# Two layer norms behind expert layers: some statistics moved to ScalarE, mean and gain in one VectorE operation

## The chip, the cores and the metric

One core of a Trainium2 chip runs the whole program. The metric is the device time of one execution in microseconds. The engines are TensorE (PE in the profile), VectorE (DVE), ScalarE (ACT), GpSimd (POOL) and SyncE (SP), which issues transfers; each runs its own instructions in program order, and they wait for one another by semaphores.

## What is computed

The reference is a decoder trunk of two layers over 1040 tokens (16 meta tokens and 1024 of the input) of width 1024. Layer 0 mixes by a convolution and a sparse attention, layer 1 by a gated recurrence. Behind each mixer comes a routed expert layer, and everything is wrapped in a norm behind the sum:

```python
for layer in range(DEPTH):
    m = conv_sparse_attn_mixer(h, ...) if layer % 2 == 0 else rglru_mixer(h, ...)
    h = layer_norm(DN_ALPHA * h + m, ln_mix_g[layer], ln_mix_b[layer])
    f = hierarchical_moe(h, ...)
    h = layer_norm(DN_ALPHA * h + f, ln_ffn_g[layer], ln_ffn_b[layer])
return h[:, N_META:]

def layer_norm(x, g, b):
    mu = jnp.mean(x, axis=-1, keepdims=True)
    var = jnp.mean(jnp.square(x - mu), axis=-1, keepdims=True)
    return (x - mu) * lax.rsqrt(var + LN_EPS) * g + b
```

The two norms with `ln_ffn` are those of this change.

## The kernel before

The program is a row of stages with a barrier of all engines between them. The expert layers leave their sums (already `h + f / ALPHA`) in DRAM; `combine` reads them in blocks of 128 tokens and norms them. It is called twice in `trunk`:

- c0 (L2712), behind layer 0's experts: nine blocks (the first has 16 tokens, the others 128), `turned` is true. The normed rows are stored and also transposed by TensorE, and each transposed block is split into a high part (`high`, ScalarE, L2386) and a low part (`low`, VectorE, L2354) for the products of the next stage. The two halves of the PSUM that take the transposes are used in turn (`TURN_SETS` = 2), so the transposes of block n wait for `low` of block n - 2. ScalarE and GpSimd also split the first two weight tiles of the recurrence (`odd.split_hi`, L2274, and `odd.split_lo`, L2278), and TensorE does the 24 steps (three matmuls each) of odd tile 0 between and behind the transposes (`STEPS_BEHIND`, L2256): 4 steps behind each of blocks 5, 6 and 7, 12 behind block 8. Steps 8 to 15 wait for `low` of block 6, steps 16 to 23 for that of block 8. The recurrence begins when all engines are through.
- c1 (L2721), the end of the kernel: eight blocks of 128 tokens, `turned` is false. The normed rows are the output.

The rows of the first two blocks are loaded ahead of the barrier, the others as the stage begins (L1738). For block n, VectorE does two `bn_stats` of 512 columns (L2333), `bn_aggr` (L2335) and adds EPS (L2336); ScalarE takes the root (`root`, L2378); VectorE takes the reciprocal (L2340) and -mean times it (L2341, together `scale`); ScalarE computes x * scale + bias in place (`centre`, L2382); VectorE multiplies by the gain, which ScalarE has copied to PSUM (`gain`, L2346, with L2389); GpSimd adds the bias (L2408); SyncE stores the rows (L2323). In c1 VectorE adds the bias of the last block itself (L2350, from a copy in PSUM, L2391).

The order is written out by hand. In turn n of its loop VectorE does stats(n), scale(n - 1), gain(n - 2) and, in c0, low(n - 4). ScalarE does root(n), centre(n - 1) and, in c0, high(n - 3). `Chain.link` makes VectorE wait for its own small results.

Of the kernel before, what the change touches and what calls it, by code (L numbers as in the profile page):

```python
# [14 lines left out]
ALU = mybir.AluOpType  # L15
ACT = mybir.ActivationFunctionType
# [7 lines left out]
P = 128  # L24
D = 1024
# [19 lines left out]
ALPHA = float(4 ** 0.25)  # L45
EPS = 1e-5
# [29 lines left out]
def tok0(b):  # L76

    return 0 if b == 0 else META + P * (b - 1)


def toks(b):
    return META if b == 0 else P
# [819 lines left out]
N = len(STEPS)  # L902
# [812 lines left out]
class Sums:  # L1715
# [11 lines left out]
    def gain(self, j):  # L1727
        return self.raw[:, GAIN_CHUNK, j * D:(j + 1) * D]
# [556 lines left out]
                   (hT_hi[:, k, m], hT_lo[:, k, m]), k == 0, k == KC - 1)  # L2285


def combine(nc, name, const, sums, out_d, hT_hi, hT_lo, beside=None, odd=None):


    blocks, x = sums.blocks, sums.rows
    N = len(blocks)
    turned = hT_hi is not None
    with Ctx(nc) as c:
        stat = c.sb(name + "st", [P, N, 18])
        g_ps = odd.bank[:, 6:8, :] if turned else c.ps(name + "g", [P, 2, 512])
        t_ps = [odd.bank[:, 2 + 2 * s:4 + 2 * s, :] for s in range(TURN_SETS)] if turned else [c.ps(name + "t", [P, 2, 512])]
        stored, bias_in, last_normed = c.sem(name + "so"), c.sem(name + "bin"), c.sem(name + "lnd")
        chain, padded, gain_in, var_done, root_done, scales, centred, gained, normed, t_mm, hi_d, lo_d = (
            c.sem(name + n) for n in ("ch", "pad", "gin", "vd", "rtd", "scl", "cen", "gain", "nd", "tm", "hd", "ld"))  # L2300
        block = c.block()

        def col(n, a, w=1):
            return stat[0:toks(blocks[n]), n, a:a + w]

        def turns(n):
            return t_ps[n % TURN_SETS].rearrange("p a (j n) -> p (a j) n", j=4)[:, :, 0:toks(blocks[n])]

        def hT(t, n):
            return t[:, :, tok0(blocks[n]):tok0(blocks[n]) + toks(blocks[n])]  # L2310

        @block.sync
        def _(sp):
            sums.load_rows(sp, BEHIND_CHANGE)
            if beside is not None:
                beside(sp)
            for n, b in enumerate(blocks):
                at = tok0(b) - sums.out0
                if n < N - 1 or turned:
                    sp.wait_ge(normed, n + 1)  # L2320
                else:
                    sp.wait_ge(last_normed, 1)
                sp.dma_start(out_d[at:at + toks(b), :], x(n)).then_inc(stored, 16)  # L2323
            sp.wait_ge(stored, 16 * N)

        @block.vector
        def _(dve):
            ch = Chain(dve, chain)

            def stats(n):  # L2330
                dve.wait_ge(sums.loaded[n], 16)
                for j in range(2):
                    ins = dve.bn_stats(col(n, 6 * j, 6), x(n)[:, 512 * j:512 * j + 512])  # L2333
                ch.link(ins)
                ch.link(dve.bn_aggr(col(n, 12, 2), col(n, 0, 12)))  # L2335
                dve.tensor_scalar(col(n, 14), col(n, 13), EPS / ALPHA ** 2, None, ALU.add).then_inc(var_done, 1)  # L2336

            def scale(n):
                dve.wait_ge(root_done, n + 1)
                ch.link(dve.reciprocal(col(n, 16), col(n, 15)))  # L2340
                dve.tensor_scalar(col(n, 17), col(n, 12), col(n, 16), -1.0, ALU.mult, ALU.mult).then_inc(scales, 1)  # L2341

            def gain(n):
                dve.wait_ge(centred, n + 1)
                g = g_ps[0:toks(blocks[n]), :, :].rearrange("p a n -> p (a n)")
                dve.tensor_tensor(x(n), x(n), g, ALU.mult).then_inc(gained, 1)  # L2346
                if n == N - 1 and not turned:
                    dve.wait_ge(gained, N)
                    dve.wait_ge(bias_in, 1)
                    dve.tensor_tensor(x(n), x(n), t_ps[0][:].rearrange("p a n -> p (a n)"), ALU.add).then_inc(last_normed, 1)  # L2350

            def low(n):
                dve.wait_ge(hi_d, n + 1)
                dve.tensor_tensor(hT(hT_lo, n), turns(n), hT(hT_hi, n).bitcast(F32), ALU.subtract).then_inc(lo_d, 1)  # L2354

            if turned:
                dve.memset(hT_hi[:, :, T:TP].bitcast(F32), 0.0).then_inc(padded, 1)
                dve.memset(hT_lo[:, :, T:TP].bitcast(F32), 0.0).then_inc(padded, 1)
            for n in range(N + 4):
                if n < N:  # L2360
                    stats(n)
                if 1 <= n <= N:
                    scale(n - 1)
                if n == 2:
                    dve.wait_ge(gain_in, 1)
                if 2 <= n <= N + 1:
                    gain(n - 2)
                if turned and n >= 4:
                    low(n - 4)
            if turned:  # L2370
                dve.wait_ge(padded, 2)
                dve.wait_ge(lo_d, N)

        @block.scalar
        def _(act):
            def root(n):
                act.wait_ge(var_done, n + 1)
                act.activation(col(n, 15), col(n, 14), ACT.Sqrt).then_inc(root_done, 1)  # L2378

            def centre(n):  # L2380
                act.wait_ge(scales, n + 1)
                act.activation(x(n), x(n), ACT.Identity, bias=col(n, 17), scale=col(n, 16)).then_inc(centred, 1)  # L2382

            def high(n):
                act.wait_ge(t_mm, n + 1)
                act.activation(hT(hT_hi, n), turns(n), ACT.Copy).then_inc(hi_d, 1)  # L2386

            act.wait_ge(sums.gains_loaded, 32)
            act.activation(g_ps[:].rearrange("p a n -> p (a n)"), sums.gain(0), ACT.Copy).then_inc(gain_in, 1)  # L2389
            if not turned:  # L2390
                act.activation(t_ps[0][:].rearrange("p a n -> p (a n)"), sums.gain(1), ACT.Copy).then_inc(bias_in, 1)  # L2391
            for n in range(N + 3):
                if n < N:
                    root(n)
                if 1 <= n <= N:
                    centre(n - 1)
                if turned and n in (5, N):
                    odd.split_hi(act, n // N)
                if turned and n >= 3:
                    high(n - 3)  # L2400

        @block.gpsimd
        def _(pool):
            pool.wait_ge(sums.gains_loaded, 32)
            n_here = N if turned else N - 1
            for n in range(n_here):
                pool.wait_ge(gained, n + 1)
                pool.tensor_tensor(x(n), x(n), sums.gain(1)[0:toks(blocks[n]), :], ALU.add).then_inc(normed, 1)  # L2408
                if turned and n in (4, N - 1):
                    odd.split_lo(pool, n // (N - 1))  # L2410
            pool.wait_ge(normed, n_here)
            if turned:
                pool.wait_ge(odd.lo_done, 2)

        if turned:
            @block.tensor
            def _(pe):
                for n in range(N):
                    q = toks(blocks[n])
                    pe.wait_ge(normed, n + 1)  # L2420
                    if n >= TURN_SETS:
                        pe.wait_ge(lo_d, n - TURN_SETS + 1)
                    for k in range(KC):
                        last = pe.transpose(t_ps[n % TURN_SETS][:, k // 4, (k % 4) * P:(k % 4) * P + q], x(n)[:, k * P:(k + 1) * P],
                                            const[0:q, C_ID:C_ID + q])
                    last.then_inc(t_mm, 1)
                    for i in range(sum(STEPS_BEHIND.get(m, 0) for m in range(n)), sum(STEPS_BEHIND.get(m, 0) for m in range(n + 1))):
                        if i == 0:
                            pe.wait_ge(odd.lo_done, 1)
                        if i % KC == 0:  # L2430
                            pe.wait_ge(lo_d, BLOCKS_OF[i // KC])
                        if i == 2 * KC:
                            pe.wait_ge(padded, 2)
                        last = odd.step(pe, 0, i, hT_hi, hT_lo)
                last.then_inc(odd.tile_mm, 1)
# [373 lines left out]
```

## Time and profile before

| | |
|---|---|
| median of 3 runs | 2654.3 us (2651.59 to 2655.76) |
| the profiled execution | 2650.81 us |
| its span, mean granted TensorE clock | 2649.0 us, 0.958 |
| c0, first `bn_stats` to the last `low` | 1483.76 to 1525.90 us |
| c1, first `bn_stats` to GpSimd's last addition | 2615.86 to 2642.97 us |

In the rows below a time is in microseconds from the start of the span. A line such as L2346 is the line of the kernel. An instruction's row has its start, its duration, its engine, and in brackets how long the engine had been idle and who released it. Rows with x2 merge two instructions of a kind.

### The profile page before, as it was taken

To read this page: it belongs to the slowest core of one execution; us is meant where nothing else is said; L and a number is where in the kernel's file an instruction comes from. 1 tells how busy PE (TensorE), PEld (TensorE's weight loads), DVE (VectorE), ACT (ScalarE), POOL (GpSimd) and SP (SyncE) were. 2 spreads that over 40 slices of the span, in tenths; PEclk is the share of its full clock that TensorE was granted. 3 is DMA by queue.
4 is the path that set the end of the run, shared out by engine and by line. 5 is a ranking of instruction groups with operands and counts; after the bars stand their busy time and mean duration, and the time that the engine had idled before them with its cause. 6 is when DMAs were issued, how large, how long until landed. Compare 5 with 4: busy or idle time off the path is not lost. (4 is left out here: it accounts for less than half of the span.)

```text
span 2649.0 us, 37690 instructions
## 1 busy us (share of the span) xinstructions
PE 2429.4 (92%) x12633; PEld 2077.0 (78%) x12633; DVE 2022.3 (76%) x2597; ACT 1699.5 (64%) x1819; POOL 665.4 (25%) x487
## 2 busy tenths in 40 slices
PE   8989988986988999999999599997979999999993
PEld 8869967885776888888888489996867888888882
DVE  4688775677888898898898543536789889889885
ACT  2369836766216877778777465663157777877873
POOL 0105717752012212222212412120012222222223
PEclk9999999997998999999999699998979999999996
DMA  5503333313339699999798511104359699999994
GB/s 172 135 1 96 80 99 103 105 34 113 125 109 376 233 339 362 370 345 322 278 366 307 185 49 40 41 17 162 96 206 355 229 350 363 363 372 363 370 356 151
DMA packets 115278, 565.24 MB, mean 213 GB/s; under 512 B 23520, under 2 KB 27872, under 8 KB 65904
## 3 DMA queue, kind: packets, MB, share of 16 engines
q1 hardware_dynamic: 89776, 512.19, 53.0%
q0 software_dynamic: 25408, 51.84, 7.2%
q8 instruction: 53, 0.87, 0.1%
q14 instruction: 41, 0.34, 0.0%
HBM read 574.25 MB, written 74.34 MB: 245 GB/s over the span
## 5 line engine op out<-in xcount | busy, mean ns | idle before, releaser
L2047 DVE TENSOR_TENSOR e0wlo<-e0raw,e0whi 128x2048 fp32r<-128x2048 f32 x214 | 486.6, 2289 | 68.7 <-ACT e0whi L1902 67.2
L2047 DVE TENSOR_TENSOR e1wlo<-e1raw,e1whi 128x2048 fp32r<-128x2048 f32 x208 | 472.7, 2288 | 66.6 <-ACT e1whi L1902 66.5
L1902 ACT ACTIVATE e0whi<-e0raw 128x2048 fp32r<-128x2048 f32 x214 | 409.7, 1915 | 98.1 <-PE e0u L93 42.1
L1902 ACT ACTIVATE e1whi<-e1raw 128x2048 fp32r<-128x2048 f32 x208 | 397.9, 1915 | 94.0 <-PE e1u L93 42.1
L91 PE MATMUL odd_banks<-h2T_hi,odd_w_hi 128*128 128x348 f32 x480 | 171.6, 357 | 2.2 <-PEq L123 1.7
L92 PE MATMUL odd_banks<-h2T_lo,odd_w_hi 128*128 128x348 f32 x480 | 155.2, 323 | 0.0
L93 PE MATMUL odd_banks<-h2T_hi,odd_w_lo 128*128 128x348 f32 x480 | 154.9, 323 | 0.0
L91 PE MATMUL m_y<-m_whi,m_xhi 128*128 128x512 f32 (+1 forms) x304 | 123.4, 406 | 24.1 <-DVE m_wlo L1609 22.9
L93 PE MATMUL m_y<-m_whi,m_xlo 128*128 128x512 f32 (+1 forms) x304 | 120.3, 396 | 0.0
L92 PE MATMUL m_y<-m_wlo,m_xhi 128*128 128x512 f32 (+1 forms) x304 | 120.0, 395 | 0.0
L91 PE MATMUL e0g<-e0whi,e0xh 128*128 128x512 f32 x284 | 116.1, 409 | 3.2 <-DVE e0xl L2052 3.2
L91 PE MATMUL e0u<-e0whi,e0xh 128*128 128x512 f32 x292 | 115.6, 396 | 0.0
L92 PE MATMUL e0u<-e0wlo,e0xh 128*128 128x512 f32 x292 | 115.4, 395 | 0.0
L93 PE MATMUL e0u<-e0whi,e0xl 128*128 128x512 f32 x292 | 115.3, 395 | 0.0
L91 PE MATMUL e1g<-e1whi,e1xh 128*128 128x512 f32 x276 | 112.2, 406 | 2.6 <-DVE e1xl L2052 2.6
L91 PE MATMUL e0yp<-e0whi,e0hh 128*128 128x512 f32 x280 | 113.6, 406 | 0.0
L2278 DVE TENSOR_TENSOR odd_w_lo<-odd_w_raw,odd_w_hi 128x1024 fp32r<-128x1024 f32 x18 | 22.3, 1239 | 119.5 <-ACT odd_w_hi L2274 119.5
L93 PE MATMUL e0g<-e0whi,e0xl 128*128 128x512 f32 x284 | 112.8, 397 | 0.0
L92 PE MATMUL e0g<-e0wlo,e0xh 128*128 128x512 f32 x284 | 112.8, 397 | 0.0
L91 PE MATMUL e1u<-e1whi,e1xh 128*128 128x512 f32 x284 | 112.4, 396 | 0.0
L92 PE MATMUL e1u<-e1wlo,e1xh 128*128 128x512 f32 x284 | 112.2, 395 | 0.0
L93 PE MATMUL e1u<-e1whi,e1xl 128*128 128x512 f32 x284 | 112.2, 395 | 0.0
(477 smaller groups left out, 7069.5 us busy)
## 6 DMA issues: line engine op xcount, KB each, us to landing
e0raw<-in_moe_w_gate SPq DMA_DIRECT2D x72, 1024.0 KB
e0raw<-in_moe_w_up SPq DMA_DIRECT2D x72, 1024.0 KB
e0raw<-in_moe_w_down SPq DMA_DIRECT2D x72, 1024.0 KB
e1raw<-in_moe_w_gate SPq DMA_DIRECT2D x70, 1024.0 KB
e1raw<-in_moe_w_up SPq DMA_DIRECT2D x70, 1024.0 KB
e1raw<-in_moe_w_down SPq DMA_DIRECT2D x70, 1024.0 KB
qki_w_raw<-in_w_even SPq DMA_DIRECT2D x22, 512.0 KB, 5.8
odd_w_raw<-in_w_odd SPq DMA_DIRECT2D x20, 512.0 KB, 3.5
```

Of the source, the lines that this page charges most:

```text
L91: pe.matmul(out, stat[0], mov[0], start=start, stop=False)
L92: pe.matmul(out, stat[0], mov[1], start=False, stop=False)
L93: return pe.matmul(out, stat[1], mov[0], start=False, stop=stop)
L1902: act.activation(w_hi[:, i, :], raw[:, i, :], ACT.Copy).then_inc(hi_done[i], 1)
L2047: dve.tensor_tensor(w_lo[:, i, :], raw[:, i, :], w_hi[:, i, :].bitcast(F32), ALU.subtract).then_inc(lo_done[i], 1)
L2278: eng.tensor_tensor(self.w_lo[:, n % 2, :], self.raw[:, n % 2, :], self.w_hi[:, n % 2, :].bitcast(F32), ALU.subtract).then_inc(self.lo_don ...
```

## The change

- Of every three blocks, the third (n % 3 == 2) has its statistics on ScalarE: `sums_of` copies the rows to a scratch tensor with the sum in an accumulator; `squares` turns the sum into -mean, squares x - mean with the sum in the accumulator, and takes the root.
- The others keep `bn_stats` and `bn_aggr` on VectorE. EPS is now the bias of the root on ScalarE, from a small tensor that VectorE fills once.
- `gain` now comes ahead of the scaling: one `scalar_tensor_tensor` computes (x - mean) * g (or (x + -mean) * g) and needs no root. `scale` is the reciprocal alone. ScalarE's `centre` becomes `rescale`, x times the reciprocal, and waits for both; GpSimd's addition waits for `rescale`.
- The last block of c1 is not rescaled on ScalarE: `last_rows` computes x * scale + bias on VectorE in one operation.
- The order: in turn n VectorE does stats(n), gain(n), scale(n) and, in c0, low(n - 2). ScalarE does root(n), squares(n + 1) where n % 3 == 1, rescale(n), sums_of(n + 2) where n % 3 == 0 and, in c0, high(n - 2). The copy of the bias to PSUM in c1 moves into turn 1. The first `odd.split_hi` comes behind high(3), the second behind high(6).

```diff
+LOW_BEHIND = 2
+        ours = [n for n in range(N) if n % 3 != 2]
...
             def stats(n):
                 dve.wait_ge(sums.loaded[n], 16)
                 for j in range(2):
-                    ins = dve.bn_stats(col(n, 6 * j, 6), x(n)[:, 512 * j:512 * j + 512])
-                ch.link(ins)
-                ch.link(dve.bn_aggr(col(n, 12, 2), col(n, 0, 12)))
-                dve.tensor_scalar(col(n, 14), col(n, 13), EPS / ALPHA ** 2, None, ALU.add).then_inc(var_done, 1)
+                    dve.bn_stats(col(n, 6 * j, 6), x(n)[:, 512 * j:512 * j + 512]).then_inc(halves_done, 1)
+                dve.wait_ge(halves_done, 2 * ours.index(n) + 2)
+                dve.bn_aggr(col(n, 12, 2), col(n, 0, 12)).then_inc(var_done, 1)
+
+            def gain(n):
+                g = g_ps[0:toks(blocks[n]), :, :].rearrange("p a n -> p (a n)")
+                if n in ours:
+                    dve.wait_ge(var_done, ours.index(n) + 1)
+                    dve.scalar_tensor_tensor(x(n), x(n), col(n, 12), g, ALU.subtract, ALU.mult).then_inc(gained, 1)
+                else:
+                    dve.wait_ge(act_root_done, n + 1 - sum(m < n for m in ours))
+                    dve.scalar_tensor_tensor(x(n), x(n), col(n, 17), g, ALU.add, ALU.mult).then_inc(gained, 1)
 
             def scale(n):
-                dve.wait_ge(root_done, n + 1)
-                ch.link(dve.reciprocal(col(n, 16), col(n, 15)))
-                dve.tensor_scalar(col(n, 17), col(n, 12), col(n, 16), -1.0, ALU.mult, ALU.mult).then_inc(scales, 1)
-
-            def gain(n):
-                dve.wait_ge(centred, n + 1)
-                g = g_ps[0:toks(blocks[n]), :, :].rearrange("p a n -> p (a n)")
-                dve.tensor_tensor(x(n), x(n), g, ALU.mult).then_inc(gained, 1)
...
+                if n in ours:
+                    dve.wait_ge(root_done, ours.index(n) + 1)
+                dve.reciprocal(col(n, 16), col(n, 15)).then_inc(scales, 1)
...
-            for n in range(N + 4):
-                if n < N:
+            for n in range(N):
+                if n in ours:
                     stats(n)
-                if 1 <= n <= N:
-                    scale(n - 1)
-                if n == 2:
+                if n == 0:
                     dve.wait_ge(gain_in, 1)
-                if 2 <= n <= N + 1:
-                    gain(n - 2)
-                if turned and n >= 4:
-                    low(n - 4)
+                gain(n)
+                scale(n)
+                if turned and n >= LOW_BEHIND:
+                    low(n - LOW_BEHIND)
+            if not turned:
+                last_rows(N - 1)
...
-            def centre(n):
-                act.wait_ge(scales, n + 1)
-                act.activation(x(n), x(n), ACT.Identity, bias=col(n, 17), scale=col(n, 16)).then_inc(centred, 1)
+            def sums_of(n):
+                act.wait_ge(sums.loaded[n], 16)
+                act.activation(junk[0:toks(blocks[n]), :], x(n), ACT.Copy, accum_out=col(n, 12)).then_inc(sum_done, 1)
+
+            def squares(n):
+                k, q = n // 3 + 1, toks(blocks[n])
+                act.wait_ge(sum_done, k)
+                act.activation(col(n, 17), col(n, 12), ACT.Copy, scale=-1.0 / D).then_inc(mean_done, 1)
+                act.wait_ge(mean_done, k)
+                act.activation(junk[0:q, :], x(n), ACT.Square, bias=col(n, 17), accum_out=col(n, 13)).then_inc(square_done, 1)
+                act.wait_ge(square_done, k)
+                act.activation(col(n, 15), col(n, 13), ACT.Sqrt, bias=eps[0:q, :], scale=1.0 / D).then_inc(act_root_done, 1)
...
+            def rescale(n):
+                act.wait_ge(gained, n + 1)
+                act.wait_ge(scales, n + 1)
+                act.activation(x(n), x(n), ACT.Copy, scale=col(n, 16)).then_inc(scaled, 1)
+
+            act.wait_ge(eps_in, 1)
+            for n in range(N):
+                if n in ours:
                     root(n)
-                if 1 <= n <= N:
-                    centre(n - 1)
-                if turned and n in (5, N):
-                    odd.split_hi(act, n // N)
-                if turned and n >= 3:
-                    high(n - 3)
+                if n % 3 == 1 and n + 1 < N:
+                    squares(n + 1)
+                if turned or n < N - 1:
+                    rescale(n)
+                if n % 3 == 0 and n + 2 < N:
+                    sums_of(n + 2)
+                if turned and n >= 2:
+                    high(n - 2)
+                    if n in (5, N - 1):
+                        odd.split_hi(act, n // (N - 1))
...
-                pool.wait_ge(gained, n + 1)
+                pool.wait_ge(scaled, n + 1)
```

## Rows read from the trace of the kernel before

**Rows 1.** The page: TensorE's busy time over the span.
```profile
PE 2429.4 (92%) x12633; PEld 2077.0 (78%) x12633; DVE 2022.3 (76%) x2597; ACT 1699.5 (64%) x1819; POOL 665.4 (25%) x487
```

**Rows 2.** Timeline of c1, one period: start, duration, engine, operation.
```profile
2625.84 1.28 DVE L2333 BATCH_NORM_STATS2 c1st<-e1raw 128x6 f32<-128x512 f32 x2
...
2628.91 1.28 DVE L2333 BATCH_NORM_STATS2 c1st<-e1raw 128x6 f32<-128x512 f32 x2
2629.08 2.34 POOL L2408 TENSOR_TENSOR e1raw<-e1raw 128x1024 f32<-128x1024 f32 x1 [0.73 <-DVE e1raw L2346]
```

**Rows 3.** Timeline of c1: its start, block 2's statistics, GpSimd's last additions.
```profile
2615.86 1.28 DVE L2333 BATCH_NORM_STATS2 c1st<-e1raw 128x6 f32<-128x512 f32 x2 [19.98 <-PEq L123]
...
2619.69 1.28 DVE L2333 BATCH_NORM_STATS2 c1st<-e1raw 128x6 f32<-128x512 f32 x2
...
2638.30 4.67 POOL L2408 TENSOR_TENSOR e1raw<-e1raw 128x1024 f32<-128x1024 f32 x2 [0.73 <-DVE e1raw L2346]
```

**Rows 4.** Timeline of c0, VectorE, one period.
```profile
1505.56 1.28 DVE L2333 BATCH_NORM_STATS2 c0st<-e0raw 128x6 f32<-128x512 f32 x2
1506.87 0.21 DVE L2335 BATCH_NORM_AGGREGATE c0st<-c0st 128x2 f32<-128x12 f32 x1
...
1508.63 1.22 DVE L2354 TENSOR_TENSOR h2T_lo<-odd_banks,h2T_hi 128x1024 fp32r<-128x1024 f32 x1
...
1509.76 1.27 DVE L2333 BATCH_NORM_STATS2 c0st<-e0raw 128x6 f32<-128x512 f32 x2
```

**Rows 5.** Timeline of c0: its start, and its last high, low and step.
```profile
1483.76 1.25 DVE L2333 BATCH_NORM_STATS2 c0st<-e0raw 16x6 f32<-16x512 f32 x2
...
1523.61 1.03 ACT L2386 ACTIVATE h2T_hi<-odd_banks 128x1024 fp32r<-128x1024 f32 x1 [1.77 <-PE odd_banks L2424]
...
1524.67 1.23 DVE L2354 TENSOR_TENSOR h2T_lo<-odd_banks,h2T_hi 128x1024 fp32r<-128x1024 f32 x1 [1.57 <-ACT h2T_hi L2386]
...
1529.73 0.32 PE L93 MATMUL odd_banks<-h2T_hi,odd_w_lo 128*128 128x348 f32 x1
```

**Rows 6.** Waits in c0: total us, times, longest.
```profile
DVE h2T_lo L2354 <- ACT h2T_hi L2386: 4.5, 3, 1.6
```

**Rows 7.** Groups by form: busy us, mean ns of one, idle before.
```profile
L2382 ACT ACTIVATE e0raw<-e0raw,c0st 128x1024 f32<-128x1024 f32 x8 | 9.9, 1239 | 0.7
...
L2527 ACT ACTIVATE rg_t<-rg_r,const 128x1040 f32<-128x1040 f32 x10 | 11.6, 1157 | 0.0
...
L1245 ACT ACTIVATE pr<-sm,nmx 128x1040 f32<-128x1040 f32 x8 | 9.2, 1154 | 0.0
...
L1245 ACT ACTIVATION_READ_ACCUMULATOR pr<-sm,nmx 128x1 f32 x64 | 12.3, 192 | 0.0
...
L1224 ACT ACTIVATE conv_spare<-glu 128x1040 f32<-128x1040 f32 x4 | 4.3, 1071 | 0.5 <-issue 0.2 <-DVE glu L1346 0.2
...
L2378 ACT ACTIVATE c0st<-c0st 128x1 f32<-128x1 f32 x8 | 1.6, 202 | 7.6 <-DVE c0st L2336 7.6
...
L1408 DVE SCALAR_TENSOR_TENSOR m_rows<-m_rows,m_st,m_gb 128x1024 f32<-128x1024 f32 x8 | 10.2, 1275 | 0.0
...
L2346 DVE TENSOR_TENSOR e0raw<-e0raw,odd_banks 128x1024 f32<-128x1024 f32 x8 | 9.7, 1210 | 0.0
```

**Rows 8.** TensorE at both clocks: timeline of c0, then slices: length, busy, granted clock.
```profile
1511.61 1.97 PE L2424 MATMUL odd_banks<-const,e0raw 128*128 128x128 f32 x8 [2.66 <-POOL e0raw L2408]
...
1514.54 0.49 PE L92 MATMUL odd_banks<-h2T_lo,odd_w_hi 128*128 128x348 f32 x1
...
1514.83 0.49 PE L93 MATMUL odd_banks<-h2T_hi,odd_w_lo 128*128 128x348 f32 x1
...
1522.54 1.04 PE L2424 MATMUL odd_banks<-const,e0raw 128*128 128x128 f32 x8
...
338.00:340.00 2.00, 0.27 (x2) 1.00 0.00 0
...
342.00:344.00 2.00, 0.00 (x0) 0.71 0.00 0
```

More of the change, by code:

```diff
@@ L2295, in combine @@
         stat = c.sb(name + "st", [P, N, 18])
+        junk, eps = c.sb(name + "junk", [P, D]), c.sb(name + "eps", [P, 1])
+        ours = [n for n in range(N) if n % 3 != 2]
         g_ps = odd.bank[:, 6:8, :] if turned else c.ps(name + "g", [P, 2, 512])
@@ L2298, in combine @@
         stored, bias_in, last_normed = c.sem(name + "so"), c.sem(name + "bin"), c.sem(name + "lnd")
-        chain, padded, gain_in, var_done, root_done, scales, centred, gained, normed, t_mm, hi_d, lo_d = (
-            c.sem(name + n) for n in ("ch", "pad", "gin", "vd", "rtd", "scl", "cen", "gain", "nd", "tm", "hd", "ld"))
+        padded, gain_in, eps_in, halves_done, var_done, sum_done, mean_done, square_done = (
+            c.sem(name + n) for n in ("pad", "gin", "epi", "hvd", "vd", "smd", "mnd", "sqd"))
+        root_done, act_root_done, scales, scaled, gained, normed, t_mm, hi_d, lo_d = (
+            c.sem(name + n) for n in ("rtd", "ard", "scl", "scd", "gain", "nd", "tm", "hd", "ld"))
         block = c.block()
@@ L2327, in _ @@
         def _(dve):
-            ch = Chain(dve, chain)
             def stats(n):
@@ L2343, in gain @@
-            def gain(n):
-                dve.wait_ge(centred, n + 1)
-                g = g_ps[0:toks(blocks[n]), :, :].rearrange("p a n -> p (a n)")
-                dve.tensor_tensor(x(n), x(n), g, ALU.mult).then_inc(gained, 1)
[L2347 to L2350, printed above, removed]
+                    dve.bn_stats(col(n, 6 * j, 6), x(n)[:, 512 * j:512 * j + 512]).then_inc(halves_done, 1)
@@ new lines, in scale, with last_rows @@
+            def scale(n):
+                if n in ours:
+                    dve.wait_ge(root_done, ours.index(n) + 1)
+                dve.reciprocal(col(n, 16), col(n, 15)).then_inc(scales, 1)
+            def last_rows(n):
+                dve.wait_ge(gained, N)
+                dve.wait_ge(scales, N)
+                dve.wait_ge(bias_in, 1)
+                dve.scalar_tensor_tensor(x(n), x(n), col(n, 16), t_ps[0][:].rearrange("p a n -> p (a n)"), ALU.mult, ALU.add
+                                         ).then_inc(last_normed, 1)
@@ L2354, in low @@
                 dve.tensor_tensor(hT(hT_lo, n), turns(n), hT(hT_hi, n).bitcast(F32), ALU.subtract).then_inc(lo_d, 1)
+            dve.memset(eps[:], EPS / ALPHA ** 2).then_inc(eps_in, 1)
             if turned:
@@ L2358, in _ @@
                 dve.memset(hT_lo[:, :, T:TP].bitcast(F32), 0.0).then_inc(padded, 1)
-            for n in range(N + 4):
-                if n < N:
+            for n in range(N):
+                if n in ours:
                     stats(n)
-                if 1 <= n <= N:
-                    scale(n - 1)
-                if n == 2:
+                if n == 0:
                     dve.wait_ge(gain_in, 1)
-                if 2 <= n <= N + 1:
-                    gain(n - 2)
-                if turned and n >= 4:
-                    low(n - 4)
+                gain(n)
[4 more added lines that the diff above has]
+                last_rows(N - 1)
             if turned:
+                for n in range(N - LOW_BEHIND, N):
+                    low(n)
                 dve.wait_ge(padded, 2)
@@ L2376, in root @@
             def root(n):
-                act.wait_ge(var_done, n + 1)
-                act.activation(col(n, 15), col(n, 14), ACT.Sqrt).then_inc(root_done, 1)
-            def centre(n):
-                act.wait_ge(scales, n + 1)
-                act.activation(x(n), x(n), ACT.Identity, bias=col(n, 17), scale=col(n, 16)).then_inc(centred, 1)
+                act.wait_ge(var_done, ours.index(n) + 1)
+                act.activation(col(n, 15), col(n, 13), ACT.Sqrt, bias=eps[0:toks(blocks[n]), :]).then_inc(root_done, 1)
+            def sums_of(n):
[9 more added lines that the diff above has]
+                act.activation(col(n, 15), col(n, 13), ACT.Sqrt, bias=eps[0:q, :], scale=1.0 / D).then_inc(act_root_done, 1)
             def high(n):
@@ L2389, in _ @@
             act.activation(g_ps[:].rearrange("p a n -> p (a n)"), sums.gain(0), ACT.Copy).then_inc(gain_in, 1)
[L2390 to L2393, printed above, removed]
-                    root(n)
-                if 1 <= n <= N:
-                    centre(n - 1)
-                if turned and n in (5, N):
-                    odd.split_hi(act, n // N)
-                if turned and n >= 3:
-                    high(n - 3)
+            def rescale(n):
[5 more added lines that the diff above has]
+                if n in ours:
+                    root(n)
+                if n % 3 == 1 and n + 1 < N:
[8 more added lines that the diff above has]
+                        odd.split_hi(act, n // (N - 1))
+                elif not turned and n == 1:
+                    act.activation(t_ps[0][:].rearrange("p a n -> p (a n)"), sums.gain(1), ACT.Copy).then_inc(bias_in, 1)
+            if turned:
+                high(N - 2)
+                high(N - 1)
         @block.gpsimd
```

## The prediction

> **What bounds the kernel now.** I read the page's engine busy times first: TensorE is busy for 92% of the span [rows 1]. That share belongs to the projections and experts. The change touches only the two `combine` calls, c0 (behind layer 0's experts) and c1 (the end), so I read the timelines of these two stretches and asked which engine never rests.
>
> In c1 it is VectorE: its next `bn_stats` starts 3.07 us after the last one, without a gap, while GpSimd rests 0.73 us before each of its additions [rows 2]. Eight blocks at that pace, then GpSimd's last two additions back to back, end at 2642.97 [rows 3]. The chain of the end is VectorE's work and then GpSimd's, so what VectorE saves in c1 shortens the kernel.
>
> In c0 a period is 4.20 us, because each turn also has a `low` of 1.22 us (L2354) [rows 4]. VectorE waits for ScalarE before `low` only three times, 4.5 us together [rows 6]; these are the last three blocks. The last `low` ends at 1525.90, and TensorE's last step of odd tile 0 ends 4.15 us later, at 1530.05; everything behind it waits for that [rows 5].
>
> **What the change removes and adds on VectorE.** Per block with its own statistics go the operation that adds EPS (L2336), the product of mean and scale (L2341) and the plain product with the gain (1.21 us, L2346). In their place comes one `scalar_tensor_tensor` with a column pointer. The nearest row is L1408, the same operation with both tensors in SBUF, at 1.275; with the gain in PSUM and no pointer it is 1.21 [rows 7]. I take 1.275 (same kind), with 1.21 as the lower end. A turn of VectorE is then: 1.31 from the first `bn_stats` to the aggregate [rows 4], 0.24 for the aggregate and its wait, 1.20 for the product (0.08 overlaps its successor), 0.07 for the reciprocal: 2.8 us. A third block needs only 1.3 us. The `memset` of eps is under 0.1 us, once.
>
> **On ScalarE.** The rescale keeps one pointer: 1.16 us for 1040 elements (L2527), so about 1.14 for 1024, against 1.24 now (the upper end) [rows 7]. The next instruction starts 0.10 before its end: 1.04. Each third block adds a sum (an ACTIVATE of about 1.14 with its accumulator read of 0.19 [rows 7], 1.12 in the queue), and then a small copy, a square (1.07 for 1040 elements without the accumulator, 1.15 for an ACTIVATE with it), a read and a root, each waiting for the one before: 1.7 us [rows 7]. GpSimd's addition now follows the rescale, with the same 2.35 us.
>
> **c1.** Laid out in program order with these durations: blocks 0 and 1 take VectorE 2.81 us each from 2615.9; block 2 is 2.58 (VectorE waits 1.3 for the square's root, since ScalarE does root 1, mean, square and root one after another); blocks 3 to 5 are 2.81 + 2.81 + 2.58 = 8.2 where three blocks now are 9.2; blocks 6 and 7 are 2.81 and 2.9; the last scale-and-add is 1.28. VectorE ends at 2639.3 and GpSimd's seventh addition at 2639.2, against 2642.97: **-3.7 us**. What is late next is all three engines together (GpSimd alone needs 7.0 of the 8.2). The row loads are no limit: block 2's rows were there at 2619.7, where VectorE read them without a wait [rows 3], and ScalarE wants them at 2619.9.
>
> **c0.** Here I find a new ring, because `low` moves from four blocks behind to two and `high` from three to two. In turn n ScalarE's queue is root(n), rescale(n), `high`(n-2), and rescale(n) waits for VectorE's product and reciprocal of the same turn. VectorE's next instruction is `low`(n-2), which waits for `high`(n-2). Behind this `low` on VectorE stand the statistics and product of n+1, and for those ScalarE, GpSimd and TensorE wait. So the two engines take turns instead of overlapping. A turn becomes 1.31 + 0.24 + 1.20 + 0.18 (reciprocal and hand-over), then ScalarE's 1.04 (rescale) and 1.05 (`high`, 1.03 [rows 5], and hand-over), then 1.14 (`low`): 6.16. With the sum ahead of `high` (n = 3, 6) it is 6.16 + 1.12 = 7.28. With the square ahead of the rescale (n = 4, 7) the rescale starts 1.70 instead of 1.38 after the aggregate: 6.47. Without statistics (n = 5, 8) it is 4.61. Three turns: 18.4 us, against 12.6 now. GpSimd and TensorE have slack: a block's transposes end before ScalarE comes to its `high`.
>
> From 1483.8: turns 0 and 1 are 2.81 each, turn 2 is 4.23 (`low`(0) is short), turns 3 to 8 are 2 x 18.4: `low`(6) ends at 1530.5. Then TensorE's steps 8 to 11, which wait for it (12 matmuls at 0.16, 1.9), transposes of block 8 (1.04 [rows 8]), `high` and `low` with hand-overs (2.4): the last `low` ends at 1535.8 instead of 1525.9: **+9.9 us**. The same way of laying out the kernel before gives 1525.94 for that `low` and 2642.85 for GpSimd's last addition, 0.1 from the trace.
>
> **TensorE's clock in c0.** At the low level (0.50 granted, 1.2 GHz) a transpose group of eight takes 1.97 us and matmuls start 0.29 apart; at the high one (2.4 GHz) 1.04 and 0.16 [rows 8]. In the laid-out c0 TensorE works from 1525.1 to 1530.5 for only 1.0 us. Elsewhere it had 0.27 us of work in a 2 us slice at 1.00, and in the slice that began 2 us behind that one, without work, the grant fell (0.71) [rows 8]. I expect a fall here too: steps 8 to 11 then take 3.5 instead of 1.9, the transposes up to 1.97 instead of 1.04: **+2.5 us**, and by the time of the last eight steps TensorE has worked long enough to be back. The Trainium skill's page "TensorE: Matmul & The Clock Gate", section "Part 1: The HAM clock gate", says it this way: "the default state is throttled, and activity releases the throttle"; it speaks against a change that spreads TensorE's work thinner, and by a reading without it the time would be 2.5 us less.
>
> **Sum.** -3.7 + 9.9 + 2.5 = +8.7. The profiled execution took 2650.8 us, so its like would take 2659.5; the median of the three runs is 3.5 us above it, so the forecast is 2654.3 + 8.7 = **2663.0**. Bounds of the single costs: rescale 1.24 (+0.8 in c0, +0.2 in c1), product 1.21 (-0.4, and -0.3 in c1), accumulating ACTIVATEs 0.1 either way (0.5 either way): about 1.5 us down or up.
>
> **Rivals.** (A) The grant doesn't fall: 2660.5. For: matmuls come back after at most 3.3 us of rest. (B) It falls and stays low through the last eight steps: 24 matmuls at 0.29 instead of 0.16, +3.1: 2666.1. (C) The other side: VectorE never waits in `low`, since `high` is there early. Then c0 is bound by VectorE's own work, 10.5 per three turns instead of 12.6, some -5.9, and with c1's -3.7 it is 2644.7. It decides from the point where three turns take less than about 13.8 us, where c1's gain pays for them. Against it stand the two queues in program order; for it, that three of nine `low`s wait today although they are farther behind. (D) ScalarE loads a table for the square and again for the root: five squares with two loads of 1.28 each are +12.8, 2675.8. Against: the four squares at L1224 ran in a stretch without a load [rows 7], though beside other functions than the root. The Trainium skill's page "ScalarE: Activation LUTs", section "Table sets: the hidden batching unit", says that cheap functions lie in every set, which speaks against D too, but it names copy and not square among them. (E) c1 gives nothing: 2666.7. (F) The ring is real but half hidden: about 2657.
>
> **Chances.** Forecast 0.45, A 0.22, B 0.10, C 0.05, D 0.03, E 0.07, F 0.08. What a measurement of this kernel can tell from no change is about 0.2%, 5.3 us: slower begins at 2659.6. The runs spread over 4 us, so 0.03 of the forecast and 0.10 of A may fall inside: slower 0.42 + 0.12 + 0.10 + 0.03 + 0.07 = 0.74, within 0.07 + 0.10 + 0.03 = 0.20, faster 0.06. The range reaches from F's and the cheap end of A, 2655.5, to the dear end of B, 2668.5; C and D stay out.
>
> **What would show it.** Right: in c0 VectorE idle for about 2.1 us before most `low`s, released by ScalarE's `high`, 3.3 where a sum stands between; last `low` near 1536 to 1538; a granted clock under 1.00 around 1530. In c1 GpSimd nearly without rest, its end near 2639 on the clock of before (plus c0's loss), and 1.3 us of VectorE's idle before the products of blocks 2 and 5. Wrong: `low` waits under 0.5 us, a second ACT_TABLE_LOAD in either call, or c0's length (from the first `bn_stats` to the last `low`) under 45 us.

## The result, and the profile after

| | before | after |
|---|---|---|
| median | 2652.93 us (2651.59 to 2655.76, 6 runs) | 2663.31 us (2659.66 to 2666.23, 6 runs) |
| ratio | | 1.0038 (95% interval 1.0028 to 1.0049) |
| the profiled execution, its span | 2650.81, 2649.0 us | 2664.29, 2662.1 us |
| c0, first `bn_stats` to the end of the last `low` | 42.1 us | 55.8 us |
| c0, first `bn_stats` to VectorE's first operation of the next stage | 48.1 us | 61.7 us |
| c1, first `bn_stats` to the last operation of any engine | 27.1 us | 24.3 us |
| from there to the end of the span | 6.0 us | 5.8 us |

The change makes the kernel 10.4 us slower: c0 loses 13.7 us, and c1 with what stands behind it gains 3.1. The spans of the two profiled executions differ by 13.1; the 2.5 us beyond the stages named lie in stages that the change doesn't touch: the recurrence with the output projection (430.0 and 431.3 us from the next stage's start to layer 1's first expert block) and the experts of layer 1 (616.0 and 617.7), less 0.5 ahead of c0. In the other profiles below these two vary between 429.7 and 432.3 and between 615.9 and 617.7, whatever was done to c0 and c1. I therefore compare the stages by their own lengths, which come from one profiled execution of each kernel, and the whole by medians. One execution below, of the kernel with c1 alone, took 2818.7 us where the ten others took 2644.6 to 2653.7, and is left out.

Turns 3 and 4 of c0, from the timeline of the changed kernel (start, duration, engine, operation, in brackets how long the engine had rested and who released it); they answer to [rows 4]:

```profile
1493.77 1.28 DVE L2338 BATCH_NORM_STATS2 c0st<-e0raw 128x6 f32<-128x512 f32 x2
...
1495.08 0.21 DVE L2340 BATCH_NORM_AGGREGATE c0st<-c0st 128x2 f32<-128x12 f32 x1
1495.33 0.29 ACT L2392 ACTIVATE c0st<-c0st,c0eps 128x1 f32<-128x1 f32 x1 [1.80 <-DVE c0st L2340]
1495.33 1.28 DVE L2346 SCALAR_TENSOR_TENSOR e0raw<-e0raw,c0st,odd_banks 128x1024 f32<-128x1024 f32 x1
1496.52 0.16 DVE L2354 RECIPROCAL c0st<-c0st 128x1 f32<-128x1 f32 x1
...
1496.77 1.15 ACT L2416 ACTIVATE e0raw<-e0raw,c0st 128x1024 f32<-128x1024 f32 x1 [1.15 <-DVE c0st L2354]
1497.83 1.04 ACT L2396 ACTIVATE c0junk<-e0raw 128x1024 f32<-128x1024 f32 x1
...
1498.78 0.19 ACT L2396 ACTIVATION_READ_ACCUMULATOR c0junk<-e0raw 128x1 f32 x1
1498.87 1.00 ACT L2409 ACTIVATE h2T_hi<-odd_banks 128x1024 fp32r<-128x1024 f32 x1
1499.90 1.22 DVE L2365 TENSOR_TENSOR h2T_lo<-odd_banks,h2T_hi 128x1024 fp32r<-128x1024 f32 x1 [3.22 <-ACT h2T_hi L2409]
1501.05 1.27 DVE L2338 BATCH_NORM_STATS2 c0st<-e0raw 128x6 f32<-128x512 f32 x2
...
1506.56 1.23 DVE L2365 TENSOR_TENSOR h2T_lo<-odd_banks,h2T_hi 128x1024 fp32r<-128x1024 f32 x1 [2.61 <-ACT h2T_hi L2409]
1507.70 1.27 DVE L2349 SCALAR_TENSOR_TENSOR e0raw<-e0raw,c0st,odd_banks 128x1024 f32<-128x1024 f32 x1
...
1511.23 1.22 DVE L2365 TENSOR_TENSOR h2T_lo<-odd_banks,h2T_hi 128x1024 fp32r<-128x1024 f32 x1 [2.19 <-ACT h2T_hi L2409]
1512.38 1.28 DVE L2338 BATCH_NORM_STATS2 c0st<-e0raw 128x6 f32<-128x512 f32 x2
```

Read it along VectorE: reciprocal at 1496.52, then nothing until `low` at 1499.90. (L2338 and L2340 are the statistics, L2346 and L2349 the product with the gain, L2354 the reciprocal, L2365 `low`; L2392 is the root, L2416 the rescale, L2396 the sum, L2409 `high`.) In these 3.22 us ScalarE does the rescale of block 3, the sum for block 5 and only then `high` of block 1, whose transposes had ended at 1496.2. ScalarE in its turn had rested 1.15 us before the rescale, for VectorE's reciprocal. The two engines work in turns. Three turns take 18.6 us (1493.77 to 1512.38), where [rows 4] show 4.20 for one.

The waits of that stretch (total us, times, longest); the first answers to [rows 6], 4.5 us in 3 times:

```profile
DVE h2T_lo L2365 <- ACT h2T_hi L2409: 23.0, 9, 4.8
...
ACT e0raw L2416 <- DVE c0st L2354: 8.3, 6, 2.6
```

c1, the same timeline, one period of three blocks; it answers to [rows 2]:

```profile
2640.89 1.27 DVE L2338 BATCH_NORM_STATS2 c1st<-e1raw 128x6 f32<-128x512 f32 x2
...
2643.70 1.27 DVE L2338 BATCH_NORM_STATS2 c1st<-e1raw 128x6 f32<-128x512 f32 x2
...
2647.98 1.28 DVE L2349 SCALAR_TENSOR_TENSOR e1raw<-e1raw,c1st,c1g 128x1024 f32<-128x1024 f32 x1 [1.38 <-ACT c1st L2405]
2649.06 6.98 POOL L2444 TENSOR_TENSOR e1raw<-e1raw 128x1024 f32<-128x1024 f32 x3 [1.38 <-ACT e1raw L2416]
...
2649.25 1.26 DVE L2338 BATCH_NORM_STATS2 c1st<-e1raw 128x6 f32<-128x512 f32 x2
```

A turn of VectorE is 2.81 us instead of 3.07, and three blocks are 8.36 us (2640.89 to 2649.25) although it rests 1.38 before block 5's product, for the root that ScalarE takes (L2405). GpSimd adds three blocks in 6.98 us without a rest between them and rests 1.38 ahead of the three.

### The profile page after: what moved, and what is told of

Read it like the earlier page. It is cut to its first block and busy times, and to the rows that moved or that the text cites. A ratio compares the mean times of both kernels' runs of the same rounds, so it can differ in the third digit from the quotient of the medians.

```text
span 2662.1 us, 37685 instructions
## 1 busy us (share of the span) xinstructions
PE 2433.8 (91%) x12633; PEld 2079.6 (78%) x12633; DVE 2011.5 (76%) x2550; ACT 1708.5 (64%) x1843; POOL 665.6 (25%) x487
## 5 line engine op out<-in xcount | busy, mean ns | idle before, releaser
L1902 ACT ACTIVATE e0whi<-e0raw 128x2048 fp32r<-128x2048 f32 x214 | 409.8, 1915 | 98.8 <-PE e0u L93 42.1
L1902 ACT ACTIVATE e1whi<-e1raw 128x2048 fp32r<-128x2048 f32 x208 | 397.9, 1914 | 94.4 <-PE e1u L93 42.1
```

The source lines that it names most:

```text
L1902: act.activation(w_hi[:, i, :], raw[:, i, :], ACT.Copy).then_inc(hi_done[i], 1)
```

## The experiments

My theory: in c0, `low`(n - 2) waits for a `high` that stands behind the rescale of the same turn, and this ring sets the pace; the fall of TensorE's clock at its end adds 2.5 us; c1 gains by itself. The rivals are that the added work on ScalarE, or the longer way of a block through rescale, GpSimd and TensorE, is what costs, that the loss comes from elsewhere, and that the clock costs nothing on the path. Every time of a whole kernel below is a median, and every ratio is to the kernel before on the same chip.

### Low three blocks behind

```diff
-LOW_BEHIND = 2
+LOW_BEHIND = 3
```

> The changed kernel with one constant: low follows three blocks behind in c0 instead of two. Theory (ring: VectorE waits in low(n-2) for ScalarE's high(n-2), which is queued behind rescale(n), which waits for VectorE's product of the same turn): low(n-3) finds its high done, VectorE works nearly without rest; c0 from the first bn_stats to the last low falls from 55.8 us to about 41 (before: 42.1), VectorE's wait for high from 23 us to under 5; the whole is about 14 us under the changed kernel, 2649, or 4 us under the kernel before. Rival (the added work on ScalarE and the longer way through rescale, GpSimd and TensorE is what costs, wherever low stands): c0 stays over 50 us and the whole near 2660.

Measured: 2649.42 us, ratio to before 0.9987 (0.9978 to 0.9996). The `low`s and the waits of c0 in this kernel, from the view of the tile (count, ns min/median/max, first and last start) and the waits:

```profile
L2365 DVE TENSOR_TENSOR h2T_lo<-odd_banks,h2T_hi x9: 272/1224/1226, 1495.1 to 1523.3; 128x1024 fp32r<-128x1024 f32 x8, 128x128 fp32r<-128x128 f32 x1
```

```profile
DVE h2T_lo L2365 <- ACT h2T_hi L2409: 7.5, 5, 3.1
```

With c0's first `bn_stats` at 1483.5 the last `low` ends 41.0 us later. One constant gives back 14.7 us of c0 and makes the kernel slightly faster than before. The wait is 7.5 us, not under 5 as I wrote, most of it still at the last blocks. The rival is out: ScalarE's work, the rescale and GpSimd's place are all as in the changed kernel.

### Low two blocks behind, high ahead of the rescale

The same ring, cut at its other end; in c1 nothing changes.

```diff
+                if turned and n >= 2:
+                    high(n - 2)
+                    if n in (5, N - 1):
+                        odd.split_hi(act, n // (N - 1))
                 if turned or n < N - 1:
                     rescale(n)
                 if n % 3 == 0 and n + 2 < N:
                     sums_of(n + 2)
-                if turned and n >= 2:
-                    high(n - 2)
-                    if n in (5, N - 1):
-                        odd.split_hi(act, n // (N - 1))
-                elif not turned and n == 1:
+                if not turned and n == 1:
```

> The changed kernel with low still two blocks behind; only ScalarE's order in c0 differs: high(n-2) (and the weight split behind it) stands ahead of rescale(n) and sums_of(n+2) instead of behind them. Theory (it is the order of high behind rescale that makes the ring, not the number two): low(n-2) finds its high done while VectorE is at its product; c0 to the last low 43 us (45 if TensorE's clock falls), the whole about 2652. Rival (two blocks are too few for the way through GpSimd and TensorE): c0 over 50 us, as now.

Measured: 2653.12 us, ratio 0.9998 (0.9989 to 1.0008), c0 43.0 us to the last `low`. So two blocks behind costs little in itself (0.8 us over the kernel before, 2.0 over three blocks behind); the large loss comes only with `high` queued behind a rescale that waits for VectorE. The rival is out. By the stages the whole should be 2.2 us under the kernel before; the interval of the ratio, 2.9 under to 2.1 over, can't tell. (VectorE waits 10.3 us for `high` here, against 23.0.)

### Each call alone

c1 of the changed kernel with c0 of the kernel before, and the other way round; the diff is the call:

```diff
-                    combine(nc, "c0", const, sums, h2_d, hT_hi, hT_lo, beside=load_odd, odd=odd)
+                    combine_old(nc, "c0", const, sums, h2_d, hT_hi, hT_lo, beside=load_odd, odd=odd)
```

> c0 as in the kernel before, c1 as in the changed one. Theory (c1's new order is a gain by itself, 27.1 to 24.3 us): about 2.8 us under the kernel before, 2650. Rival (the end is set by the last stores, c1 gives nothing): no difference from before, 2653.

Measured: 2649.8 us, ratio 0.9988 (0.9979 to 0.9998); c1 24.3 us, c0 42.0.

> c0 as in the changed kernel, c1 as in the kernel before. Theory (all of the loss is in c0): 13 to 14 us over the kernel before, 2666, with c0's length 55.8 us to the last low. Rival (part of the loss comes from elsewhere, such as the expert layer, which was 2.3 us longer in the changed kernel's profile): under 11 us over before.

Measured: 2666.70 us, ratio 1.0051 (1.0036 to 1.0066); c0 54.6 us, c1 27.1. Together -3.0 and +13.9, against +10.4 for both: the loss is all in c0, the gain all in c1, and they add up within the noise. c0 is 1.2 us shorter here than in the changed kernel, with the same code; the part on the clock below shows why.

### The statistics of the third block back on VectorE

```diff
-        ours = [n for n in range(N) if n % 3 != 2]
+        ours = list(range(N))
```

(and no `squares` and `sums_of`)

> The changed kernel with every block's statistics on VectorE again (no sums_of and squares); order, rescale and the single product stay. Theory (the ring costs the same either way, since in it the sum and the square on ScalarE take what the statistics take on VectorE): c0 to the last low 56 us, c1 24.8 instead of 24.4, the whole 2663 to 2664. Rival (the load of statistics on ScalarE is what makes c0 slow): c0 under 50 us, the whole under 2658.

Measured: 2663.65 us, ratio 1.0046 (1.0030 to 1.0061); c0 55.8 us, c1 24.5. The part of the change that its name puts first does nothing measurable, in either direction. What c1 gains comes from the rest of the change: mean and gain in one operation, the two small operations of VectorE gone, and the order that this allows, together; no run separates these.

### TensorE's clock

In the changed kernel (slices of c0: length, TensorE busy, granted clock):

```profile
1522.00:1524.00 2.00, 2.00 (x14) 1.00 0.00 0
1524.00:1526.00 2.00, 0.05 (x1) 1.00 0.00 0
1526.00:1528.00 2.00, 1.28 (x6) 0.64 0.27 109
1528.00:1530.00 2.00, 0.69 (x4) 0.50 0.38 154
1530.00:1532.00 2.00, 0.88 (x3) 0.50 0.00 0
...
1536.00:1538.00 2.00, 2.00 (x13) 0.80 0.00 0
```

The grant falls after a slice with 0.05 us of work, and comes back in the slice from 1536, when TensorE had worked since 1531.12. Steps 8 to 11 and the transposes of block 8 run at the low level, from the timeline:

```profile
1531.12 0.66 PE L91 MATMUL odd_banks<-h2T_hi,odd_w_hi 128*128 128x348 f32 x1 [2.44 <-DVE h2T_lo L2365]
...
1534.77 1.91 PE L2460 MATMUL odd_banks<-const,e0raw 128*128 128x128 f32 x8
```

To price this, matmuls on constant data were added where TensorE rests:

```diff
                     last.then_inc(t_mm, 1)
+                    for _ in range(20 if n == 7 else 0):
+                        pe.matmul(odd.bank[:, 0, 384:512], const[:, C_ID:C_ID + P], const[:, C_ID:C_ID + P], start=True, stop=True)
...
                         last = odd.step(pe, 0, i, hT_hi, hT_lo)
+                    for _ in range(16 if n == 6 else 0):
+                        pe.matmul(odd.bank[:, 0, 384:512], const[:, C_ID:C_ID + P], const[:, C_ID:C_ID + P], start=True, stop=True)
```

> The changed kernel plus 36 small matmuls (128 columns, constant data, into free columns of a finished PSUM bank, their result unused) on TensorE in c0: 16 behind step 7, 20 behind the transposes of block 7, where TensorE would rest until block 7 and low(6). Theory (the granted clock falls in these rests and puts 1.7 us on steps 8 to 11 and 0.9 on the transposes of block 8, which lie on the path): the grant stays at 1.00 from 1522 on, steps 8 to 11 take 1.9 us instead of 3.65, c0 to the last low falls from 55.8 to about 53.2 us, the whole from 2663.3 to about 2660.7. Rival (these steps are hidden behind the ring, or the added matmuls stand in its way): c0 stays at 55.8 or grows.

Measured: 2665.39 us, ratio 1.0043 (1.0029 to 1.0056), c0 55.8. The second half of the rival came: the grant stayed at 1.00 in every slice from 1526 to the end of c0, but the added work stood in the way.

```profile
1533.30 4.63 PE L2464 MATMUL odd_banks<-const 128*128 128x128 f32 x40
...
1537.68 0.41 PE L91 MATMUL odd_banks<-h2T_hi,odd_w_hi 128*128 128x348 f32 x1
```

Twenty matmuls are forty rows and 4.63 us; `low`(6) had ended at 1535.1, and step 8 began at 1537.68. The 2.5 us won at the high clock were lost by the late start. So I took fewer, 7 behind step 7 and 13 behind the transposes of block 7.

> As the kernel with added matmuls on TensorE, but 7 behind step 7 and 13 behind the transposes of block 7. In the kernel with 16 and 20 the grant stayed at 1.00 and steps 8 to 11 took 2.0 us, but 20 matmuls (each runs as two rows of 0.116 us) took 4.63 us and ended 2.6 us after low(6), so that the steps began that much late. Theory (the clock's fall costs 2.5 us on the path): the 20 now fit into the rests, steps 8 to 11 begin with the end of low(6), c0 from the first bn_stats to the last low is 53.2 us instead of 55.8, the whole 2.5 us under the changed kernel, near 2661. Rival (the fall costs nothing on the path): c0 stays at 55.8.

Measured: 2662.71 us, ratio 1.0036 (1.0023 to 1.0050), c0 53.3 us to the last `low`.

```profile
1524.00:1526.00 2.00, 2.00 (x17) 1.00 0.00 0
1526.00:1528.00 2.00, 0.94 (x9) 1.00 0.00 0
1528.00:1530.00 2.00, 1.92 (x17) 1.00 0.58 238
...
1532.00:1534.00 2.00, 1.59 (x10) 1.00 0.27 96
```

```profile
1532.49 0.42 PE L91 MATMUL odd_banks<-h2T_hi,odd_w_hi 128*128 128x348 f32 x1 [0.41 <-DVE h2T_lo L2365]
...
1534.50 1.03 PE L2460 MATMUL odd_banks<-const,e0raw 128*128 128x128 f32 x8
```

Steps 8 to 11 take 2.01 us instead of 3.65, the transposes 1.03 instead of 1.91, and c0 is 2.5 us shorter. By the stage's length the clock's price is shown. The median of the changed kernel (2663.3, on another occasion) is too near to show it, but the next kernel below, which keeps the low clock (steps 8 to 11 in 3.65 us), ran beside this one on the same chip: 2664.95, 2.2 us more, and all five executions of this one were shorter than all four of that one. Their c0s differ by 2.1.

The price isn't the same in every execution. In the profile of the kernel with c0 alone, whose c0 has the same code as the changed kernel's:

```profile
1528.99 1.47 PE L2460 MATMUL odd_banks<-const,e0raw 128*128 128x128 f32 x8 [2.36 <-POOL e0raw L2444]
...
1533.39 0.66 PE L91 MATMUL odd_banks<-h2T_hi,odd_w_hi 128*128 128x348 f32 x1 [2.94 <-DVE h2T_lo L2365]
...
1536.75 1.04 PE L2460 MATMUL odd_banks<-const,e0raw 128*128 128x128 f32 x8
```

The grant fell only during the transposes of block 7 and was back before the end of steps 8 to 11: these took 3.36 us (0.3 less than in the changed kernel) and the transposes of block 8 1.04 (0.9 less). That is the 1.2 us by which this c0 was shorter; `low`(6) ends 47.8 us behind the first `bn_stats` in both. The clock cost 1.4 us here where it cost 2.5 there.

### The table load

Ahead of its first root ScalarE loads a table (ACT_TABLE_LOAD). In the kernel before this load follows the copy of the gain without a wait, 0.95 us behind the first `bn_stats`:

```profile
1484.71 1.28 ACT L2378 ACT_TABLE_LOAD   x1
```

In the changed kernel it stands behind the wait for the first statistics, 1.57 us behind the first `bn_stats`:

```profile
1484.80 1.28 ACT L2392 ACT_TABLE_LOAD   x1 [0.67 <-DVE c0st L2340]
...
1486.09 0.29 ACT L2392 ACTIVATE c0st<-c0st,c0eps 16x1 f32<-16x1 f32 x1
...
1486.42 0.15 DVE L2354 RECIPROCAL c0st<-c0st 16x1 f32<-16x1 f32 x1 [0.31 <-ACT c0st L2392]
```

```diff
+            act.activation(warm[:], const[:, C_ROW:C_ROW + 1], ACT.Sqrt)
             act.wait_ge(eps_in, 1)
```

> The changed kernel with a root of a constant column as ScalarE's second instruction in both calls. Theory (in the changed kernel the table load stands behind the wait for the first statistics, 0.6 to 0.7 us of rest, and puts the first reciprocal off): the load follows the copy of the gain at once; c0 to the last low 55.4 instead of 55.8, c1 24.0 instead of 24.4, the whole 0.8 us less, which the timing can hardly tell from none; the trace decides. Rival: the first reciprocal waits for something else and the lengths stay.

Measured: 2664.95 us, ratio 1.0051 (1.0035 to 1.0066); c0 55.4 us, c1 24.2.

```profile
1486.58 1.03 ACT L2413 ACTIVATE odd_banks<-e0raw 128x1024 f32<-128x1024 f32 x1 [11.43 <-PEq L123]
1487.63 1.28 ACT L2419 ACT_TABLE_LOAD   x1
1488.92 0.20 ACT L2419 ACTIVATE c0warm<-const 128x1 f32<-128x1 f32 x1
```

The load follows the copy without a rest. It is worth 0.4 us in c0, and in c1 only 0.1 of the 0.4 expected: c1's first turn is 0.39 us shorter (2.92 instead of 3.31), but blocks 3 to 5 take 8.66 us instead of 8.36, because ScalarE's rescale of block 3 starts 0.39 us behind the end of the reciprocal instead of 0.10. The best version below shows the same; why, no run shows. The medians can't show either.

### A version that beats both

`LOW_BEHIND` = 3, the early table, and ScalarE's order in c0:

```diff
             for n in range(N):
+                if turned and n >= 3:
+                    high(n - 3)
+                    if n in (5, N - 1):
+                        odd.split_hi(act, n // (N - 1))
                 if n in ours:
                     root(n)
...
-                if turned and n >= 2:
-                    high(n - 2)
-                    if n in (5, N - 1):
-                        odd.split_hi(act, n // (N - 1))
...
             if turned:
+                high(N - 3)
                 high(N - 2)
```

> The changed kernel with low three blocks behind, high three behind and at the head of ScalarE's turn, and a root of a constant column as ScalarE's second instruction in both calls, so that the table is loaded before the first statistics are there instead of behind the wait for them. Theory (both engines then work nearly without rest in c0, and each call starts 0.4 us earlier): c0 to the last low 39.2 us, c1 24.0, the whole 6 us under the kernel before, 2646.5, and 3 us under the kernel with low three behind alone. Rival (VectorE or GpSimd already set the pace there): no better than 2649.4.

Measured: 2645.95 us (2642.16 to 2650.87, 8 runs) beside 2653.25 for the kernel before, ratio 0.9978 (0.9967 to 0.9988); c0 39.0 us, c1 24.2, VectorE's wait for `high` 5.8 us.

> The same as the kernel with both orders and the early table, with every block's statistics on VectorE. Theory (the third block's statistics on ScalarE are worth nothing in c0 and 0.4 us in c1, because ScalarE is as full as VectorE): c0 to the last low 39.0 us, c1 24.4, the whole within 1 us of the kernel with the third block on ScalarE. Rival (taking a third of the statistics off VectorE is worth its 1.5 us a block, 4 us in c0 and 3 in c1): 5 us or more slower than it.

Measured: 2646.13 us, ratio 0.9974 (0.9965 to 0.9983); c0 39.1 us, c1 24.1. The two can't be told apart, so in the best order, too, the third block's statistics on ScalarE bring nothing. The busy time in the same 18 us of c0, first with them on ScalarE, then on VectorE (PE, PEld, DVE, ACT, POOL, then the grant and DMA):

```profile
1498.00:1516.00 18.00, 12.29 (x59) 11.30 (x59) 14.56 (x21) 16.31 (x24) 13.47 (x7) 0.58 0.59 240
```

```profile
1501.00:1519.00 18.00, 12.95 (x63) 12.15 (x64) 16.66 (x26) 13.01 (x16) 13.32 (x7) 0.59 0.62 253
```

The fullest engine is ScalarE in the one (16.3 us) and VectorE in the other (16.7): the move changes which engine is full, and not how full.

## Why the prediction was right, point by point

**The whole.** Forecast 2663.0, measured 2663.3. That this is so near is partly luck: the sum, +8.7, was 1.7 short of the +10.4 measured, and its base, the median of three runs, was 1.4 above the median of six. By the stages, c0 was to lose 12.4 and lost 13.7, and c1 was to gain 3.7 and gained 3.1.

**What bounds c0 and c1.** Right for the kernel before: VectorE set the pace in both. The version with both orders and every block's statistics on VectorE shows it: with mean and gain in one operation and the two small ones gone it takes 3.1 us from c0 and 3.0 from c1. In the best version VectorE is no longer alone; taking more off it brings nothing.

**The ring.** Right in mechanism and nearly in size. Forecast for turns 3 to 5: 7.28, 6.47, 4.61, together 18.4. Measured from the starts of VectorE's first operation in each turn: 7.28, 6.65, 4.68, together 18.6. The rests before `low` were to be 3.3 with a sum between, and 2.1 without; they are 3.22 and 2.19, and 2.61 in the turn with a square. The surplus in turn 4, 0.18, fits the two roots that stand in it, each with EPS as a pointer bias: 0.29 us where I took the 0.20 of the root without one [rows 7]. Undone from either end (constant 3, or `high` ahead), the ring is gone.

**The start of c0 and c1.** Missed: nothing in my sum moved the table load. It came 0.6 us later, behind the wait for the statistics, and the first reciprocal with it: turn 0 is 3.27 us where I had 2.81. The early table gives back 0.4 us in c0. That, the longer roots and hand-overs make `low`(6) end 47.8 us after the first `bn_stats` (1531.07 - 1483.23), where I had 46.7. The last `low` ends at 1539.0, 1 us behind the 1536 to 1538 that I gave as a sign.

**The clock.** Right: +2.5 expected, 2.5 shown by the added matmuls. That the size is so near is partly luck, as the same code paid 1.4 in another profile. The place of the fall was a few us off: in the changed kernel it came before the transposes of block 7 (1526.72, 1.97 us), which don't lie on the path. It was back for the last eight steps (24 matmuls started within 3.8 us), so rival B didn't come. The quoted sentence of the Trainium skill's page "TensorE: Matmul & The Clock Gate", section "Part 1: The HAM clock gate", agrees with the traces: the grant stood at 0.50 in c0 from 1506 to 1518, where TensorE worked 3.0 of 12 us, and fell behind the slice with 0.05 us of work; keeping TensorE at work kept it at 1.00.

**c1.** The mechanism was right, the size too large: 27.1 to 24.3 us and 0.3 less behind it, -3.1, where I had -3.7. Two terms were mis-sized: the first turn, 3.31 us instead of 2.81 (the first reciprocal waits for the late table load), and each period of three blocks, 8.36 instead of 8.20 (it, too, has two of the longer roots).

**The rivals.** A and F didn't come. C, on the other side, is what the kernel with constant 3 does: c0 below its old length. I had set it at 2644.7 with VectorE never waiting, and its real form is 2649.4 with 7.5 us of waits left. D is out: each of the two calls has one table load of 1.28 us, though the square runs between roots. The Trainium skill's page "ScalarE: Activation LUTs", section "Table sets: the hidden batching unit", doesn't name the square among the cheap functions of every set; the trace shows that square and root need no second load here. E is out by the run with c1 alone.

**What the change was for.** I laid c1 out with the third block on ScalarE and had 2.58 us for that block instead of 2.81, with a 1.3 us rest in it. What I didn't draw from it is that the move itself is then worth next to nothing; the runs without it show that. (Three blocks take 8.36 us; three turns of 2.81 are 8.43.)

## What to carry to other kernels

When a stage is pipelined over several in-order engines, write down for each turn what stands ahead of the awaited instruction in its engine's queue: a distance of two blocks is enough if nothing in that queue waits for the same turn's work, and too short if something does. A reordering that shortens the common path for one caller of a helper (c1) should be laid out separately for every caller, because here the same order lost over four times as much in c0 as it gained in c1. And before work is moved from one engine to another, look for the wait that it brings with it and compare both engines' time per block: in c1 the 1.5 us of statistics taken off VectorE came back as a 1.38 us wait for ScalarE's root, and in c0, in the best order, ScalarE became about as full as VectorE had been.

## What the runs showed of the hardware that I had not expected

A plain matmul of float32 constants, 128 columns, is two rows of 0.116 us at the high clock (40 rows in 4.63 us), 0.23 us in all, while a transpose of the same size is one row of 0.13 (eight in 1.03). A root of a single column takes 0.20 us without a pointer bias and 0.29 with one. The table load stands directly in front of c0's first root in the profiles shown, but not always on the same side of that root's wait: the kernel before had it ahead (0.95 us behind the first `bn_stats`), the changed one, with a second wait and a pointer bias, behind (1.57 us). Which of the two moves it, no run separates.
